# A 256-column score product moved ahead of another unit's transposes in differential attention

## The reference, cut to what matters

```
s1 = einsum('bhqd,bhkd->bhqk', q1, k1) * scale      # q1, k1: 64 numbers a head
s2 = einsum('bhqd,bhkd->bhqk', q2, k2) * scale
a  = softmax(s1) - lam * softmax(s2)
o  = einsum('bhqk,bhkd->bhqd', a, v)                # v: 128 numbers a head
```

## Time and profile before

| | us |
|---|---|
| median of three runs | 1027.92 |
| span of the profiled execution | 1031.95, on the page 1032.0 |
| time of the profiled execution | 1033.59 (the only one of the three that is longer than this span) |
| TensorE matmul busy | 955.5 (93%) |
| VectorE / ScalarE / GpSimd busy | 516.5 / 330.3 / 395.3 |
| attention, from the first score product to the end of the last unit's products | about 180 to 269 |
| one attention step in the steady part | 4.42 |

### The profile page before, as it was taken

One profiled execution on the slowest core, in us unless ns is written; L12 is line 12 of the kernel. 1 busy time (PEld: TensorE's weight loads), 2 busy tenths in 40 slices (PEclk: granted clock), 3 DMA queues, 4 the chain that ended last, 5 costly groups with the idle time before them and its releaser, 6 DMA issues.

```text
span 1032.0 us, 13915 instructions
## 1 busy us (share of the span) xinstructions
PE 955.5 (93%) x4003; PEld 395.9 (38%) x4004; DVE 516.5 (50%) x697; ACT 330.3 (32%) x594; POOL 395.3 (38%) x298
## 2 busy tenths in 40 slices
PE   4899999899999989979999898996999999999796
PEld 1644444466555543323333232332333333333232
DVE  1246775777156954443544344542545445444345
ACT  4112231377245422222233222332132332322232
POOL 0313331000000044654555644655456565556520
PEclk9899999999999999989999899999899999999898
DMA  9945551800314957999989999999999999999945
GB/s 371 354 183 205 196 200 61 347 2 1 123 81 157 361 222 285 394 390 380 379 312 321 389 385 377 377 370 348 391 392 346 369 350 361 385 350 374 342 142 181
DMA packets 62541, 298.04 MB, mean 289 GB/s; under 512 B 14590, under 2 KB 15330, under 8 KB 34481
## 3 DMA queue, kind: packets, MB, share of 16 engines
q1 hardware_dynamic: 42722, 260.11, 63.8%
q0 software_dynamic: 18736, 35.41, 14.2%
q10 hardware_dynamic: 1056, 2.18, 0.6%
HBM read 282.15 MB, written 38.27 MB: 310 GB/s over the span
## 4 chain that ended last, share of the span: by engine, by line
PE 48%; DMA 40%; SPq 4%; issue 3%; DVE 3%; ACT 1%; POOL 1%; ACTq 0%; DVEq 0%; POOLq 0%
DMA wring<-in_w_e_down 33%; PE psum L972 12%; PE psum L1214 11%; PE psum L1226 5%; DMA wring<-in_w_e_up 5%; PE psum L1062 3%; PE psum L1042 3%; PE psum L1009 3%; DMA heads<-in_w_ada 3%; PE psum L1033 2%; SPq L463 2%; PE psum L1176 2%; PE psum L952 2%; SPq L439 1%; PE psum L1309 1%
## 5 line engine op out<-in xcount | busy, mean ns | idle before, releaser
L1214 PE MATMUL psum<-wring,xres 128*64 x832 | 379.0, 609 | 36.1 <-DVE cur_g L1669 34.1
L1214 PE MATMUL psum<-cur_g,xres 128*64 128x512 f32 x832 | 379.0, 609 | 0.0
L567 POOL DMA_INDIRECT xg<-h_rows,gidx x216 | 249.1, 1153 | 209.6 <-ACT gidx L813 136.7
L1214 PEld LDWEIGHTS psum<-wring,xres 128*64 128x64 f32 x832 | 112.3, 140 | 259.1 <-issue 254.1
L1673 DVE STREAM_TRANSPOSE xres<-xg 128x1024 f32<-128x1024 f32 x53 | 108.4, 2046 | 166.1 <-DMA xg<-h_rows,gidx 163.3
L1226 PE MATMUL psum<-wring,rows 128*64 x416 | 188.7, 597 | 1.9 <-ACT rows L809 1.9
L1226 PE MATMUL psum<-rows 128*64 128x512 f32 x416 | 188.7, 597 | 0.0
L1669 DVE COPY cur_g<-wring 128x1536 f32 x106 | 126.5, 1235 | 44.3 <-SPq L452 40.4
L574 POOL DMA_INDIRECT expert_sums<-xres,sidx x50 | 87.6, 1751 | 94.9 <-DMA expert_sums<-xres,sidx 82.3
L871 ACT COPY xres<-psum 128x1024 f32<-128x1024 f32 x52 | 52.6, 1012 | 201.0 <-DMA expert_sums<-xres,sidx 108.3
L1214 PEld LDWEIGHTS psum<-cur_g,xres 128*64 128x64 f32 x832 | 112.2, 140 | 0.0
(11 more groups left out here) (254 smaller groups left out, 912.7 us busy)
## 6 DMA issues: line engine op xcount, KB each, us to landing
wring<-in_w_e_gate SPq DMA_DIRECT2D x64, 1024.0 KB
wring<-in_w_e_up SPq DMA_DIRECT2D x64, 1024.0 KB
wring<-in_w_e_down SPq DMA_DIRECT2D x64, 1024.0 KB
ring<-in_w_ada SPq DMA_DIRECT2D x20, 1024.0 KB, 5.1
ring<-in_w_in SPq DMA_DIRECT2D x3, 2048.0 KB, 25.8
heads<-in_w_ada SPq DMA_DIRECT2D x4, 1024.0 KB, 23.2
ring<-in_w_out SPq DMA_DIRECT2D x1, 4096.0 KB, 15.1
acc<-expert_sums SPq DMA_DIRECT2D x8, 512.0 KB, 8.2
```

The lines of the kernel that those rows point to most:

```text
L567: pool.indirect_dma_start(xg[q][:, 256 * s:256 * s + 256], None, hrows, bass.IndirectOffsetOnAxis(gidx[:, q, s:s + 1].bitcast(U32), 0), bo ...
L1214: last = pe.matmul(pp[2][SUB * g:SUB * g + SUB, 512 * q:512 * q + 2 * F] .rearrange("p (u f) -> p u f", u=2), xT[:, q, k, SUB * g:SUB * g ...
```

## The change

`scores(u)` is split. `open_scores(u)` has its waits and product B; `close_scores(u)` has A, C, the wait on `s_scs`, and D. In step k the opening of unit k+1 stands before the transposes of unit k-2, and the closing after them, where all four products stood. `scores(0)` and `scores(1)` become an opening and a closing with nothing between. The products themselves, their operands and their places in PSUM stay the same, and no other engine's program changes.

```
-            def scores(u):
+            def open_scores(u):
                 ... (the waits on s_rope, s_ipe, s_poolout)
                 if u >= 2:
                     pe.wait_ge(s_exp, 2 * (u - 1))
+                score_product(u, 1, 0, 256).then_inc(s_scs, 1)
+
+            def score_product(u, s, c0, n):
+
                 t, h = divmod(u, HEADS)
-                for s, c0, n in ((0, 0, 512), (1, 0, 256), (1, 256, 512), (0, 512, 256)):
-                    o0 = 2 * KEYS * (u % 2) + KEYS * s + c0
-                    if (s, c0) == (0, 512):
-                        pe.wait_ge(s_scs, u + 1)
-                    last = pe.matmul(psum[:, o0:o0 + n], ...)
-                    if (s, c0) == (1, 0):
-                        last.then_inc(s_scs, 1)
-                last.then_inc(s_sc, 1)
+                o0 = 2 * KEYS * (u % 2) + KEYS * s + c0
+                return pe.matmul(psum[:, o0:o0 + n], ...)
+
+            def close_scores(u):
+
+                score_product(u, 0, 0, 512)
+                score_product(u, 1, 256, 512)
+                pe.wait_ge(s_scs, u + 1)
+                score_product(u, 0, 512, 256).then_inc(s_sc, 1)
...
-            scores(0)
-            scores(1)
+            for u in range(2):
+                open_scores(u)
+                close_scores(u)
             modulation_rows()
             for k in range(1, UNITS + 2):
+                if k + 1 < UNITS:
+                    open_scores(k + 1)
                 if k >= 2:
                     turn_probabilities(k - 2)
                 if k + 1 < UNITS:
-                    scores(k + 1)
+                    close_scores(k + 1)
```

More of the change, by code:

```diff
@@ L1003, in scores @@
                     pe.wait_ge(s_exp, 2 * (u - 1))
+                score_product(u, 1, 0, 256).then_inc(s_scs, 1)
+            def score_product(u, s, c0, n):
                 t, h = divmod(u, HEADS)
-                for s, c0, n in ((0, 0, 512), (1, 0, 256), (1, 256, 512), (0, 512, 256)):
-                    o0 = 2 * KEYS * (u % 2) + KEYS * s + c0
-                    if (s, c0) == (0, 512):
-                        pe.wait_ge(s_scs, u + 1)
-                    last = pe.matmul(psum[:, o0:o0 + n], qT[64 * s:64 * s + 64, h, t * P:(t + 1) * P],
-                                     kT[64 * s:64 * s + 64, h, c0:c0 + n], start=True, stop=True)
-                    if (s, c0) == (1, 0):
-                        last.then_inc(s_scs, 1)
-                last.then_inc(s_sc, 1)
+                o0 = 2 * KEYS * (u % 2) + KEYS * s + c0
+                return pe.matmul(psum[:, o0:o0 + n], qT[64 * s:64 * s + 64, h, t * P:(t + 1) * P],
+                                 kT[64 * s:64 * s + 64, h, c0:c0 + n], start=True, stop=True)
+            def close_scores(u):
[3 more added lines that the diff above has]
+                score_product(u, 0, 512, 256).then_inc(s_sc, 1)
             def turn_probabilities(u):
```

## The result

The changed kernel took 1033.99 us in the median of six runs (1028.97 to 1035.3), beside 1028.7 (1026.58 to 1033.59) for six runs of the kernel before. The ratio is 1.0038, 95% interval 1.002 to 1.0057, so about 3.9 us slower. Twelve further runs on another occasion gave 1.0025 (1.0004 to 1.0046), 2.6 us. Both lie on the slow side of the +0.9 us that was forecast. The first median lies outside the stated range of 1025.8 to 1032.6; the median of the twelve, 1030.74, lies inside it.

A forecast was written before the change was run, and what follows sets the result against it. TensorE was taken to bound the kernel (busy 93% of the span, 4.23 of 4.42 us a step). Terms -0.68 + 1.11 + 0.5 = +0.9 us on the median of 1027.92 gave 1028.8 us, range 1025.8 to 1032.6 (8 in 10).

The forecast's parts named there:

- The steady step: Attention steps 3 to 14: 4.46 us instead of 4.42, +0.04 each, +0.5 us in all.
- The first two rivals: Array-mode changes dearer or D gains nothing: 1030.5 to 1033.2 us, chance 0.14; changes cost nothing: 1023.2 us, chance 0.08.
- Units 0 and 1: Products up to the first modulation row: 2.77 us instead of 3.45 with B first, -0.68 us.
- The order of step 2: Unit 0's transposes move from idle time to behind the wait for unit 1's exponentials: 4.26 us against 3.15, +1.11.
- the sum: Whole kernel: -0.68 + 1.11 + 0.5 = +0.9 us.
- the fourth rival: Near step 2, longer TensorE idle time brings a second slow-clock stretch costing 1.3 us; 1030.1 us, chance 0.10.
- The third rival: The opening's wait for the exponentials decides in every step, at most 1.11 us each; 1041.6 us, chance 0.03.

The follow-up runs named there:

- the fifth experiment: B-first kernel plus an extra 256-column product ahead of the transposes in steps 3 to 14: half-array 0.9990, 4.46 us a step; full-array 0.9953, 4.11.
- the filled kernel: Changed kernel plus three extra unused full-array products in TensorE's idle time at the head of step 2; ratio 0.9988 to the kernel before, attention 87.8 us.
- the filled kernel before: Kernel before plus two extra unused full-array products ahead of unit 0's transposes, in the idle time; ratio 1.0017 to the kernel before, attention 86.9 us.
- all three traces with the new step 2: Changed kernel twice (1.0038, 1.0025), and B moved ahead of the transposes in step 2 alone, elsewhere B first behind them (0.9970), against the kernel before.
- The B-first kernel: Kernel before with B put first of the four products, all still behind the transposes; ratio 0.9955 to the kernel before, attention 81.9 us.
- the change but in step 2: Changed kernel, except that step 2 keeps its transposes ahead of B; ratio 0.9995 to the kernel before, attention 86.4 us.

## Why the prediction was wrong

The steady step was right. 4.46 us was forecast and the chain gives 4.46. B comes 0.21 behind `attend`, the transposes 0.62 behind B (0.63 forecast), 1.49 from A to `attend`, and the fourth transpose no longer waits. Twelve steps of +0.04 cost 0.5 us together. The first two rivals, on the changes of array mode, did not occur: the passage there and back costs 0.35 us a step in the fifth experiment, as the rows had it.

Units 0 and 1 were right: 2.78 us up to the first modulation row (180.33 - 177.55) against the 2.77 forecast (its terms add up to 2.78) and 3.45 before.

The order of step 2 was right. In the filled kernel, at full clock, it takes 2.91 us from B to `attend` (196.82 - 193.91), and 0.63 + 0.61 + 0.20 + 1.49 = 2.93 was forecast. Counted from the first score product, `attend` of unit 0 starts 0.4 us later than in the filled kernel before (18.95 and 18.53), as the text had listed.

So the sum was right at full clock. The changed kernel with its idle time filled takes 87.8 us of attention, the kernel before with its own filled 86.9: +0.9, as forecast.

The step that failed is step 2's clock. The text priced step 2 at full speed, and left a longer slow stretch to the fourth rival, "The clock falls for longer near step 2", with a chance of 0.10 and 1.3 us. This rival occurred in all three traces with the new step 2: with 3.07 us of idle time instead of 1.92, the stretch is 6.83 us long instead of 3.41. The filled kernels give the price of each stretch: 2.9 to 3.0 us in the changed kernel (90.7 and 90.8 to 87.8) and 1.5 to 1.6 in the kernel before (88.4 and 88.5 to 86.9). That is less than half of 6.83, in part because its first 0.64 us fall into the idle time. So the longer stretch costs 1.4 us, near the 1.3 of the rival, and 0.9 + 1.4 = 2.3 us is what the attention of the traces lost; the ratios mean 3.9 and 2.6. The text had the row with the slow `attend` in front of it and had worked out that the idle time would grow to 3 us. It should have charged the growth to the forecast, not to a rival.

The range was too tight in another way. Even with the fourth rival the sum gives 1030.1, and the first six runs have a median of 1033.99. Of the difference, 0.8 us are the kernel before, whose median rose from 1027.92 to 1028.7 with three more runs; for the rest no trace gives a cause, and the next twelve runs came back to 1030.74. Their ratio of 1.0025 has an interval that holds the 0.9 us that was forecast (1.0009). Single runs of the kernel before lie between 1023.87 and 1033.59 over all occasions, so a median of six can be 2 us off.

The third rival did not occur: the exponentials end 0.34 ahead of B in the steady part, which is the 0.29 of the forecast and 0.05 for the way to TensorE.

One thing is open: a stretch of 3.41 us disappears from the traces of the kernel before when the idle time is filled, but no time is gained, and the runs do not say why. So the clock's price is shown in the attention of the traces, and less firmly in the times: filling the idle time of the changed kernel took its ratio from 1.0025 to 0.9988, on different chips, with intervals that just overlap. The B-first kernel gains 6.5 us in the attention of its traces, which its time allows (4.6, 2.7 to 6.7).

## What to carry to other kernels

A product that uses half the array's rows was free here beside one that uses the other half, and costs two changes of mode (0.35 us here) where it stands alone among full-array work: filling an idle 0.19 us with it made a busier engine and a longer step. When one of four products waits for another's semaphore, first ask which order sets it early; that alone gave 0.33 us a step. A wait moved ahead of work that ran in idle time should be costed at the first steps too, where it lengthens an idle time, and with the clock that follows it.

## What the runs showed of the hardware

- In the kernel before, the semaphore that B sets in one half of the array is seen only when the earlier product A in the other half is done: B's record ends at 221.20, A's second pass at 221.63, and D's weight load starts at 221.69. With B first there is no such wait.
- Idle time and slow clock are not in simple proportion. After 1.92 us of idle TensorE the kernel before has 3.41 us at 1.2 GHz in each trace. After 2.26 us the B-first kernel has none in two traces, nor have its two variants of the fifth experiment and the change but in step 2:

```profile
190.79 0.88 PE L1031 MATMUL psum<-cst,ring 128*128 128x128 f32 x6
193.93 1.56 PE L1010 MATMUL psum<-heads 64*128 64x256 f32 x8 [2.26 <-ACT ring L690]
195.42 1.60 PE L1038 MATMUL psum<-heads,ring 128*128 128x128 f32 x12
```

  What sets them apart these runs do not say.
